# The first projection tiles in quarters between the modulation weights, in a two-layer mixer kernel

## The reference

```python
shift, scale, gate = ada_mod(c, ada_w[i], ada_b[i])          # silu(c) @ w + b, split in 3
h = rms_norm(x, norm_w[i]) * (1.0 + scale) + shift           # the same for ctx with c_ctx
u, v, ga, q, k, vv, gb = jnp.split(h @ w_in, AB_SPLITS, -1)  # layer 0
q = rms_norm(q, qn_w); k = rms_norm(k, kn_w)                 # per head of 128, then rotary
a_out = chunk_sgu(u, v, w_s, b_s) * jax.nn.silu(ga)
b_out = attention(q, k, vv) * jax.nn.silu(gb)
x = x + gate * (concatenate([a_out, b_out]) @ w_out)
```

## Time and profile before

| | us |
|---|---|
| median of 3 runs | 2459.89 (2455.70 to 2465.83) |
| the profiled execution: its own time / span in the trace | 2464.77 / 2463.0 |
| TensorE busy | 2351.9 (95%) |
| VectorE, ScalarE, GpSimd busy | 1088.4, 1135.8, 1172.1 (44 to 48%) |
| DMA | 143 GB/s on average; 352 MB |

### The profile page before, as it was taken

One profiled execution on the slowest core, in us unless ns is written; L12 is line 12 of the kernel. 1 busy time (PEld: TensorE's weight loads), 2 busy tenths in 40 slices (PEclk: granted clock), 3 DMA queues, 4 the chain that ended last, 5 costly groups with the idle time before them and its releaser, 6 DMA issues.

```text
span 2463.0 us, 59202 instructions
## 1 busy us (share of the span) xinstructions
PE 2351.9 (95%) x25852; PEld 1951.4 (79%) x25852; DVE 1088.4 (44%) x2330; ACT 1135.8 (46%) x2042; POOL 1172.1 (48%) x642
## 2 busy tenths in 40 slices
PE   6789999999999988999999999999999999998997
PEld 1467777777777866788888888888888888888997
DVE  1144433433440016655555555555555555553323
ACT  3333332333342227545664466545654566444443
POOL 3133333333335552466446654566447654663554
PEclk9899999999999998999999999999999999999998
DMA  9646555555535221233233332333233323336553
GB/s 400 251 149 238 195 203 183 189 204 181 210 143 196 97 94 58 90 104 105 78 105 104 113 104 80 113 104 104 86 106 104 112 80 104 104 96 239 190 182 119
DMA packets 99346, 352.14 MB, mean 143 GB/s; under 512 B 10768, under 2 KB 15248, under 8 KB 96784
## 3 DMA queue, kind: packets, MB, share of 16 engines
q1 hardware_dynamic: 99088, 348.36, 40.1%
HBM read 336.13 MB, written 12.19 MB: 141 GB/s over the span
## 4 chain that ended last, share of the span: by engine, by line
PE 81%; ACT 8%; DVE 4%; DMA 3%; issue 2%; POOL 1%; SPq 0%; ACTq 0%; DVEq 0%
PE bank L647 9%; PE bank L649 9%; PE bank L648 9%; PE bank L814 7%; PE bank L816 6%; PE bank L815 6%; PE bank L610 3%; ACT scratch L1508 3%; PE bank L1054 2%; PE bank L911 2%; PE bank L856 2%; PE bank L855 2%; PE bank L854 2%; PE bank L1056 2%; PE bank L1055 2%; PE bank L1023 2%
## 5 line engine op out<-in xcount | busy, mean ns | idle before, releaser
L448 POOL TENSOR_TENSOR wl<-raw,wh 128x1024 fp32r<-128x1024 f32 x215 | 516.8, 2411 | 624.7 <-ACT wh L443 624.6
L814 PE MATMUL bank<-hh,wh 128*128 128x512 f32 (+1 forms) x1040 | 409.6, 394 | 22.3 <-DVE hl L1755 15.4
L647 PE MATMUL bank<-hh,wh 128*128 128x512 f32 x960 | 387.0, 403 | 20.3 <-POOL wl L376 20.3
L816 PE MATMUL bank<-hh,wl 128*128 128x512 f32 (+1 forms) x1040 | 382.5, 368 | 0.0
L815 PE MATMUL bank<-hl,wh 128*128 128x512 f32 (+1 forms) x1040 | 382.4, 368 | 0.0
L648 PE MATMUL bank<-hl,wh 128*128 128x512 f32 x960 | 377.7, 393 | 0.0
L649 PE MATMUL bank<-hh,wl 128*128 128x512 f32 x960 | 377.7, 393 | 0.0
L376 POOL TENSOR_TENSOR wl<-raw,wh 128x1024 fp32r<-128x1024 f32 x82 | 200.5, 2458 | 371.3 <-ACT wh L371 371.2
L443 ACT ACTIVATE wh<-raw 128x1024 fp32r<-128x1024 f32 x232 | 245.5, 1060 | 277.8 <-PE bank L856 121.7
L814 PEld LDWEIGHTS bank<-hh,wh 128*128 128x128 f32 x1040 | 198.3, 191 | 59.3 <-issue 13.9
L647 PEld LDWEIGHTS bank<-hh,wh 128*128 128x128 f32 x960 | 182.8, 190 | 70.5 <-POOL wl L376 21.0
(11 more groups left out here) (283 smaller groups left out, 4374.0 us busy)
## 6 DMA issues: line engine op xcount, KB each, us to landing
raw<-w_in SPq DMA_DIRECT2D x256, 512.0 KB, 3.6
raw<-w_ada SPq DMA_DIRECT2D x104, 512.0 KB, 5.4
raw<-w_out SPq DMA_DIRECT2D x84, 512.0 KB, 3.7
scratch<-w_ada SPq DMA_DIRECT2D x56, 512.0 KB, 5.5
scratch<-keep_g SPq DMA_DIRECT2D x15, 1024.0 KB, 5.9
scratch<-w_in SPq DMA_DIRECT2D x26, 512.0 KB, 6.8
raw<-w_gate SPq DMA_DIRECT2D x22, 512.0 KB, 4.3
scratch<-xT SPq DMA_DIRECT2D x2, 4096.0 KB, 12.9
```

The lines of the kernel that those rows point to most:

```text
L448: eng.tensor_tensor(buffers(s)[1], raw[:, s % RAW, :], buffers(s)[0].bitcast(F32), ALU.subtract)\
L647: pe.matmul(ps, w[:, k * P:(k + 1) * P], hhv[:, kk, :], start=first and k == 0, stop=False)
L814: pe.matmul(ps, w[:, k * P:(k + 1) * P], hhv[:, kk, t0:t1], start=first and k == k0, stop=False)
L816: done = pe.matmul(ps, r[:, k * P:(k + 1) * P], hhv[:, kk, t0:t1], start=False, stop=last and k == k1 - 1)
```

## The change

1. **Six tiles in quarters.** The first six output tiles (keys, values, q and now also v of group 0) are cut in 12 pieces of 512 KB instead of 10 halves for five tiles. Piece 3p+j holds, for two output tiles, the blocks of the four feature tiles 4p to 4p+3. Nine pieces are loaded and multiplied among the modulation blocks 2 to 7 (`piece`), the last three after them. The order of the ring, of SyncE's loads, of ScalarE's and GpSimd's splits follows.
2. **The last sum inside a piece.** The sum of the last early block stands between the two halves of piece 8, and four late eighths come before the last three pieces.
3. **The third tile amid the keys' norms.** Both halves of the u tile of group 0 are multiplied between the sums and rotations of the keys. In group 0, TensorE goes from the q sum over four eighths to the ga tile, then to the rotation and the turn of v. VectorE does group 0's gate units after the norm of q and after the rotation.
4. **Norm blocks staggered.** ScalarE marks the end of the narrow activations and waits for it only ahead of the high-part copy, which comes after the next tile's narrow activations. This holds for both layers.
5. **Squares on two engines.** Even squares are added by GpSimd, odd ones by VectorE, and TensorE sums the two; the reciprocal moves ahead of the first pair of blocks. Layer 0's normalized tiles use eight buffers instead of two.

SyncE's loads, TensorE, ScalarE, VectorE and GpSimd, and the arrays' order on the host:

```diff
                     ring_load(sp, "half", h, w[h - h0, :, :])
 
             for a in range(NEARLY):
-                ada_loads(a, 0, 8)
-                for h in SOONER.get(a, ()):
-                    half_loads(w_in0, 0, h, h + 1)
-            half_loads(w_in0, 0, 5, HMIX)
+                h = 3 * (a // 2 - 1)
+                if a >= 2 and a % 2:
+                    half_loads(w_in0, 0, h + 1, h + 2)
+                ada_loads(a, 0, 3)
+                if a >= 2:
+                    half_loads(w_in0, 0, h + 2 * (a % 2), h + 2 * (a % 2) + 1)
+                ada_loads(a, 3, 8)
+            half_loads(w_in0, 0, PIECES0 - 3, PIECES0)
+            late_loads(0, 4)
+            half_loads(w_in0, 0, PIECES0, PIECES0 + 4)
 
...
             crow_load(0)
-            for n in range(GROUPS):
+            unit_loads(0)
+            late_loads(4, 8)
+            unit_loads(2)
+            late_loads(8, 12)
+            half_loads(w_in0, 0, PIECES0 + 4, PIECES0 + 6)
...
+            def first_square_sum():
+                pe.wait_ge(sem("even_added"), KT // 2 - 1)
+                pe.matmul(pb[6][:, :], ones[:, :], n_acc, start=True, stop=False)
+                pe.wait_ge(sem("odd_added"), KT // 2 - 1)
+                pe.matmul(pb[6][:, :], ones[:, :], n_odd, start=False, stop=True).then_inc(sem("n_summed"), 1)
+
...
-            def first_half(n):
-                front_half(n, pb[SOONBANK[n]][:, :], True, False, "h_lo", 0)
-
-            def second_half(n, ready=None):
-                front_half(5 + n, pb[SOONBANK[n]][:, :], False, True, ready, 1)
+            def piece(p, j, k0=0, k1=4):
+
+                h = 3 * p + j
+                if k0 == 0:
+                    pe.wait_ge(sem("front_lo"), h + 1)
+                w, r = fh[h % SPLIT], fl[h % SPLIT]
+                for k in range(k0, k1):
+                    kk = 4 * p + k
+                    pe.wait_ge(sem("h_lo"), kk + 1)
+                    for x in range(2):
+                        ps, cs = pb[SOONBANK[2 * j + x]][:, :], slice((4 * x + k) * P, (4 * x + k + 1) * P)
+                        pe.matmul(ps, w[:, cs], hhv[:, kk, :], start=(kk == 0), stop=False)
+                        pe.matmul(ps, w[:, cs], hlv[:, kk, :], start=False, stop=False)
+                        done = pe.matmul(ps, r[:, cs], hhv[:, kk, :], start=False, stop=(kk == KT - 1))
+                if k1 == 4:
+                    done.then_inc(sem("front_done"), 1)
...
                 if a >= 2:
                     pe.wait_ge(sem("mod_added"), a - 1)
+                p = a // 2 - 1
                 ada(a, 0, 3, pb[2 + a % 2])
                 if a:
                     ada_sum(a - 1, pb[2 + (a - 1) % 2])
-                if a == 2:
-                    square_sum(0)
-                if a == 6:
-                    first_half(1)
-                if a == 7:
-                    first_half(3)
+                if a == 1:
+                    first_square_sum()
+                if a >= 2 and a % 2:
+                    piece(p, 1)
                 ada(a, 3, 8, pb[2 + a % 2])
-                if a == 5:
-                    first_half(0)
-                if a == 6:
-                    first_half(2)
+                if 2 <= a < NEARLY - 1:
+                    piece(p, 2 * (a % 2))
+            piece(2, 2, 0, 2)
             ada_sum(NEARLY - 1, pb[2 + (NEARLY - 1) % 2])
-            first_half(4)
+            piece(2, 2, 2, 4)
+            pe.wait_ge(sem("mod_added"), NEARLY - 1)
+            late_ada(0, 4)
 
             def k_sum(g):
                 pe.wait_ge(sem("k_squared"), g + 1)
-                pe.matmul(pb[3 - g][:, :], ones[:, :], a_sq, start=True, stop=True).then_inc(sem("k_summed"), 1)
...
-            second_half(1)
+            piece(3, 0)
+            piece(3, 1)
             pe.wait_ge(sem("mod_added"), NEARLY)
             k_sum(0)
-            second_half(2)
+            piece(3, 2)
             k_sum(1)
-            second_half(3)
+            front_half(PIECES0, pb[0][:, :], True, False)
             pe.wait_ge(sem("mix_in"), 32)
+            pe.wait_ge(sem("kv_copied"), 2 * KVH)
             k_rotate(0)
-            second_half(4)
+            front_half(PIECES0 + 1, pb[0][:, :], False, True)
             k_rotate(1)
             vv_turn(0)
...
-                front_tile(h + 2, pb[1][:, :])
-                late_ada(PERGROUP * n, PERGROUP * n + 4)
+                    front_tile(h + 2, pb[1][:, :])
...
                 pe.wait_ge(sem("q_copied"), n + 1)
-                front_tile(h + 4, pb[0][:, :])
-                pe.wait_ge(sem("q_normed"), n + 1)
-                pe.matmul(pb[4][:, 0:SEG], ROT, a_q[:, SEG:T], start=True, stop=True).then_inc(sem("q_rotated"), 1)
+                if n:
+                    front_tile(h + 4, pb[0][:, :])
+                else:
+                    late_ada(4, 8)
+                    pe.wait_ge(sem("k_ready"), KVH)
+                    front_tile(h + 6, pb[1][:, :])
                 pe.wait_ge(sem("v_copied"), n + 1)
+                pe.wait_ge(sem("normed"), KVH + n + 1)
+                pe.matmul(pb[4][:, 0:SEG], ROT, a_q[:, SEG:T], start=True, stop=True).then_inc(sem("rotated"), 1)
                 if n:
                     pe.wait_ge(sem("a_merged"), n)
                 else:
...
                 late_ada(PERGROUP * n + 8, PERGROUP * n + 12)
 
...
+            def first_square(k):
+                if k >= 4:
+                    act.wait_ge(sem("odd_added" if k % 2 else "even_added"), k // 2 - 1)
+                dst = n_sq[k % 2] if k >= 2 else (n_acc, n_odd)[k]
+                act.activation(dst, xv[:, k, :], ACT.Square).then_inc(sem("n_squared"), 1)
...
+                    act.wait_ge(sem("h_lo"), layer * KT + k - 8 + 1)
                 full = norm_full(layer, k)
                 for s in range(2):
                     m = layer * 3 * KT + k
                     last = act.activation(full[:, s * SEG:(s + 1) * SEG], norm_t(layer, k)[:, s * SEG:(s + 1) * SEG],
                                           ACT.Identity, scale=affa[:, k, s:s + 1], bias=mod[:, m, s:s + 1])
-                    ch.link(last)
-                act.activation(hhv[:, k, :], full, ACT.Copy).then_inc(sem("h_hi"), 1)
+                    made = ch.mark(last)
+                return made
+
+            def norm_hi(layer, k, made):
+                ch.wait(made)
+                act.activation(hhv[:, k, :], norm_full(layer, k), ACT.Copy).then_inc(sem("h_hi"), 1)
+
+            def norm_group(layer, first, end):
+                made = norm_affine(layer, first)
+                for k in range(first + 1, end):
+                    later = norm_affine(layer, k)
+                    norm_hi(layer, k - 1, made)
+                    made = later
+                norm_hi(layer, end - 1, made)
 
             def ada_rows(a, bank):
...
-            for k in range(10):
-                square(0, k)
+            for k in range(KT):
+                first_square(k)
             ada_rows(0, pb[2])
-            for k in range(10, KT):
-                square(0, k)
+            norm_root(0)
             ada_rows(1, pb[3])
-            norm_root(0)
             for p in range(4):
+                front_split_hi(act, 3 * p)
                 if p == 3:
-                    front_split_hi(act, 4)
+                    front_split_hi(act, 3 * p + 1)
                 act.wait_ge(sem("aff_ready"), p + 1)
-                norm_affine(0, 4 * p)
-                norm_affine(0, 4 * p + 1)
-                if p == 2:
-                    front_split_hi(act, 1)
-                    front_split_hi(act, 2)
+                norm_group(0, 4 * p, 4 * p + 4)
                 if p < 3:
                     ada_rows(2 * p + 2, pb[2])
-                norm_affine(0, 4 * p + 2)
-                norm_affine(0, 4 * p + 3)
-                if p == 1:
-                    front_split_hi(act, 0)
-                if p == 2:
-                    front_split_hi(act, 3)
+                    front_split_hi(act, 3 * p + 1)
+                front_split_hi(act, 3 * p + 2)
                 if p < 3:
...
-            front_split_hi(act, 5)
-            front_split_hi(act, 6)
-            front_split_hi(act, 7)
             kv_copy(0)
             k_square(0)
-            front_split_hi(act, 8)
             kv_copy(1)
+            front_split_hi(act, PIECES0)
+            kv_copy(2)
             k_root(0)
+            front_split_hi(act, PIECES0 + 1)
             k_square(1)
-            front_split_hi(act, 9)
-            kv_copy(2)
-            k_root(1)
             kv_copy(3)
...
                 else:
+                    act.activation(a_q, pb[SOONBANK[4]][:, :], ACT.Copy).then_inc(sem("q_copied"), 1)
+                    k_root(1)
+                    act.activation(a_sq, pb[SOONBANK[4]][:, :], ACT.Square).then_inc(sem("q_squared"), 1)
+                    cond_row_silu(0)
+                    front_split_hi(act, PIECES0 + 2)
                     for g in range(KVH):
...
             for p in range(4):
```

(27 more changed lines are left out.)

196 lines of the change are left out of this document (112 added, 84 removed).

## The result

| | before | the change |
|---|---|---|
| median, first comparison (5 runs each) | 2458.6 | 2444.82 (2440.2 to 2447.19) |
| median, second comparison (11 and 5 runs) | 2460.61 | 2443.44 (2443.27 to 2445.7) |
| profiled execution, time / span | 2464.77 / 2463.0 | 2444.82 / 2443.0 |

The ratio of the first comparison is 0.9941 (95% interval 0.992 to 0.9961), that of the second 0.9933 (0.9921 to 0.9944): that is 14.5 and 16.5 us faster, where 30 were forecast and the range ended at 2443. Between the two profiled executions the gain is 20.0.

A forecast was written before the change was run, and what follows sets the result against it. The load queue bounds until about 60 us, then TensorE, with idles and low clock. 46.9 + 167.1 + waits 24.9 put the q sum at 238.9, 25.8 earlier; plus 4.6 gives 30.4 off 2464.77, 2434.4, median 2429.5, range 2418 to 2443.

The forecast's parts named there:

- The sum's products: TensorE's matmuls from piece 0 to group 1's q sum, at full clock without waits: 167.1 us.
- The start: Loads ahead of piece 0: 24 eighths at 1.26 us each, so TensorE reaches the piece at 46.9 us.
- (a): TensorE's waits for weights among blocks and pieces, once or twice a pair: 6.0 us, bounds 0 and 19.
- (b): Last norm block: VectorE's first scaling meets GpSimd's split, 1.4 us.
- (c): Group 0, four eighths behind the q sum: the last waits for a slot until half 15 is split, 8.1 us.
- (d): Group 0, v's norm on VectorE ahead of the scores: TensorE waits 3.6 to 4.9 us, 4.9 taken.
- (e): TensorE's lowered clock after idles: three slowdowns of 1.5 us, for (c), (d) and the worst of (a), 4.5 us.
- Stage 2: Layer 1's norm: staggering brings ScalarE's pace from 1.79 to 1.44 us per tile, a gain of 4.6 us.
- fewer waits: Rival: (c) and (d) don't appear, 11 us less, about 2418; chance 0.10.
- More hand-offs bind: Rival: each of the nine pieces waits for its low part as well, 11 us more, 2440; chance 0.16.
- slower: Rival: all nine pieces wait 8.35 us for their low part, 38.8 us slower, 2499; chance 0.04.
- the stagger gives nothing: Rival: layer 1's narrow activations take 0.60 us each, pace 1.74, 4.6 us less gain, 2434; chance 0.08.

The follow-up runs named there:

- experiment 11: The change with the odd squares added by GpSimd too, still into their own sum: median 2448.36, ratio 0.995 to the kernel before.
- experiment 4: The change with VectorE's gate units 2 and 3 of group 0 ahead of q's rotation instead of behind it: median 2438.01, ratio 0.9906 to the kernel before.
- experiment 10: The change plus experiment 8's edits, with half 16's high-part copy behind v's root in group 0: 2425.09, ratio 0.9861 to the kernel before.
- experiment 3: The change with half 15's high part copied ahead of q's root in group 0: median 2432.66, ratio 0.9886 to the kernel before.
- experiment 8: The change with half 15's copy before q's root, gate units 0, 1 before q's norm, 2, 3 behind, blocks cut after the fourth eighth: 2424.91, ratio 0.9859.
- experiment 2: The kernel before with the staggering in layer 1's norm alone: ratio 0.9978 to the kernel before, 5.4 us.

## Why the prediction missed

The places and the causes of the waits were right, the direction too; the size was not: about half of the gain came. The products took 9.3 us more than their sum, and by luck the waits, 3.1 us under theirs, hid a part of that. Against the steps:

- **The sum's products** is the step that failed: forecast at 167.1 us, measured at 176.4 (199.4 from piece 0 to the q sum, less 17.4 of idle and 5.6 of low clock). Within it it is the eighths, "Most go in runs: 0.50". From piece 0's end at 54.49 to 139.07 the change has 44 eighths and 6 block sums between pieces. Without idle they take 34.1 us; at 0.50 and 0.98 each they would take 27.9. That is 6.2 of the 9.3 us by which the q sum is later than forecast. 2.3 of the 6.2 are the cuts: five runs of three at 1.84 for 1.5, three runs of five at 2.70 for 2.5. The trace of before showed it at its own cuts of three and five; I read a run of four at 188.51, where the pairs are whole. 4.3 more are three runs in which the eighths came one by one behind their loads, each taking about 1.0 by itself, besides the idle: 4.29 and 4.16 for five, 2.85 for four. The two late loads of such a run are shown here:

```profile
107.51 1.05 PE L652 MATMUL bank<-raw,scratch 128*32 128x512 f32 x4 [0.86 <-DMA raw<-w_ada]
...
110.68 1.05 PE L652 MATMUL bank<-raw,scratch 128*32 128x512 f32 x4 [0.87 <-DMA raw<-w_ada]
```

The prediction misread such a lone eighth. Its 0.62 is a row of two records, half an eighth; a whole one has four, as the row at 69.30 with 1.05. (The block sums took 5.5 for 5.9.)
- **Pieces among eighths** take 5.66 to 5.71 us, not the 5.54 of halves in a row, and the one with a sum inside 5.82: 1.4 more for the nine.
- **The start**: 48.78 for 46.9, 1.9 more. 24 loads in a row was too smooth: a wait of 1.54 for one stands at 45.29, and the last eighth ahead of piece 0 starts at 47.80, 31.5 us behind the first, 1.31 a load instead of 1.26. It then takes 0.98 alone, not 0.5. The trace of before has both: a wait of 1.68 at 45.40, and its 27th eighth at 50.46, 1.32 a load. The queue did not stand: it moved 389 to 422 GB/s in every stretch of 1 or 2 us from 36 to 48 us of the change. That speaks against slots that TensorE emptied late; why that load landed late stays open. The squares' "I cost it at nothing" was wrong in its reason: `hl` had 1.2 us in hand (ready at 47.57), but the queue behind which I hid the second engine depends on TensorE, and experiment 11 puts it at 5 us.
- **Waits**: (a) 3.8 for 6.0, (b) 1.1 for 1.4, (c) 6.85 and 0.34 for 8.1, (d) 5.23 for 4.9: 3.1 less in all. (The top of 19 given for (a) does not follow from what stands beside it: 12 gaps of 1.5 are 18, half of them 9.) **(e) the clock**: 0.9 and 1.9 on the two slow tiles, 1.4 on the fourth eighth (1.85 us for one), 1.4 on the mixing: 5.6 for 4.5.
- Together 6.2 + 1.4 + 1.9 - 3.1 + 1.1 = 7.5 of 9.3; of the other 1.8, 1.0 is the sum of q in group 0 itself (170.76 to 171.78), which the list of small products leaves out, and the rest is spread over the others.
- **Stage 2**: 4.0 for 4.6. The pace is 1.50, not 1.44, a narrow activation 0.48. The first product came 0.9 us later behind the sum of squares, where I took off 0.6, and the wait for `wl`, taken as it is, grew by 0.5.
- **The profiled execution**: 2434.4 was forecast for it and 2444.8 measured. The rest of the miss in the median, 4.9, came of carrying over that the profiled execution of before lay above its median; the change's lay at its own.
- **Turns of VectorE and GpSimd.** VectorE's adds of squares took 1.3 us each beside GpSimd's, 2.0 a pair, and v's scaling, which reads two inputs, took 2.53 us in the change and 0.69 in experiment 4. The rule of the Trainium skill that was weighed, "SBUF — State Buffer", section "Who interferes with whom", speaks of such instructions with two SBUF inputs, and the trace agrees. The instruction of experiment 10 (2.01 against 0.17 us) has one input, so the rule as the prediction put it does not cover it; the same section also names `tensor_scalar`, which it is, among those that can contend with GpSimd.

Of the rivals, "fewer waits" was refuted by the change itself; experiments 3, 4 and 8 then took most of these waits out by other orders. "More hand-offs bind" and "slower" did not come: the nine pieces never stood for a low part. Nor did "the stagger gives nothing", by experiment 2.
